# POOL adds three of the eight rows of x, and three pairs of their squares, in three of a kernel's norms

## The chip, the cores and the metric

The kernel runs on one core of one Trainium2 chip. The metric is the device time of one execution in microseconds (us), as the median of several runs. Rows below call the engines PE (TensorE; PEld is its weight load), DVE (VectorE), ACT (ScalarE), POOL (GpSimd) and SP (SyncE, which issues the DMAs).

## The reference

Two stacks of two layers each work on `x` of 256 tokens by 1024 channels, in float32. What matters here is the first stack (`first_block`), which the text calls block 1:

```
for layer in range(DEPTH):                                  # DEPTH = 2
    h = rms_norm(x, norm_mix_pre[layer])
    m = mixer_block(h, ...)                                 # ends in merged @ w_out
    x = x + rms_norm(m, norm_mix_post[layer])
    h = rms_norm(x, norm_ffn_pre[layer])
    f = swiglu(h, w_ffn_gate[layer], w_ffn_up[layer], w_ffn_down[layer])
    x = x + rms_norm(f, norm_ffn_post[layer])

def rms_norm(x, w):
    return x * lax.rsqrt(jnp.mean(x * x, axis=-1, keepdims=True) + EPS) * w
```

Block 2 (`second_block`) takes that x. It normalises x and a context of 256 more tokens, mixes them by a convolution, an mLSTM and attention, and adds the result and a feed-forward to x, in two layers. It begins with the same kind of norm of x as stands behind block 1's mixers.

## The kernel before

**Layout.** The channels lie on the partitions: x is `xs`, 8 rows (k = 0 to 7) of 128 partitions by 512 columns, where columns 0 to 255 are the context of block 2 and 256 to 511 the tokens of x (`LAT`). `mix` and `work` have the same shape. So "a row" below is 128x256 float32, and a sum over channels is a sum over the partitions of all eight rows.

**The weight stream.** All weights come through one ring. SP loads a unit of 128x1024 float32 in two halves into `raw` (3 slots). ACT copies each half to `w_hi` in a rounded format (L1733, semaphore `hi_ready`), and POOL writes the remainder, raw minus w_hi, to `w_lo` (L1065, `lo_ready`); both have 4 slots (`SPLIT`). PE multiplies with w_hi and w_lo (L1114 to L1116, L1130, L1134) and gives a slot free. That is all that POOL does before: 624 units, two halves each, in one loop of 12 units a round (`low_part`, L1061 to L1070). ACT may split unit n only when PE is done with unit n - 4, so POOL has nothing to do while PE takes no new weights.

**A norm between two products** (the places that the change touches) goes like this, in the order in which each engine's program is written out by hand:

1. After the last tile of `w_out` or `w_ffn_down` PE sums the squares of `mix`, ACT takes the root (L1790), DVE the reciprocal (L2229), and PE spreads it over the partitions into a bank, `STAT` (L1243).
2. `add_normed` (DVE, L2386 and L2390): for each row k, work[k] = mix[k] * weight[k] * STAT; then xs[k] = xs[k] + work[k], which counts up `x_ready`. The scaling of row k+1 is written ahead of the addition of row k, and the addition waits (`dve_chain`) for its own scaled row.
3. `squares_of_x` (ACT, L1767): for each row, when `x_ready` says that it is there, work[k] = xs[k] squared, which counts up `sq_ready`. ACT's program is strictly in the order of k.
4. `norm_sums` (PE, L1304 to L1316): per row two matmuls (`token_sums`, L1230; the trace has two records for each) that add the squares over the partitions. `token_sums` waits for `sq_ready` row by row. Behind rows 1, 3 and 5 stands one `modulation_unit` (L1346, four small matmuls on other data) in the two norms behind the mixers; in the norm that begins block 2 there is none, but 4 matmuls of filler (`keep_busy`, L1158) ahead.
5. Root, reciprocal and spreading again, and then DVE, ACT and PE go through the rows of the normalised x into the next product.

The name of the norm tells the place: ("norm_mix_post", 0) and ("norm_mix_post", 1) stand behind block 1's mixers of layer 0 and 1; ("norm_ffn_post", 1) stands behind its last feed-forward and is followed by block 2's first norm. The norm behind layer 0's feed-forward has code of its own and is not touched. Below they are called the first, the second and the third norm.

Of the kernel before, what the change touches and what calls it, by code (L numbers as in the profile page):

```python
# [14 lines left out]
KD = D // P  # L15
# [3 lines left out]
CTX, LAT = (0, SEQ), (SEQ, T2)  # L19
DEPTH = 2  # L20
# [558 lines left out]


PLACE = Place()
FFN2_AT = [next(i for i, t in enumerate(TILES) if t.name == "fa" and t.layer == l) for l in range(DEPTH)]


# [41 lines left out]
def mixer_stack_kernel(nc, stream, vectors, consts, decay, gla_masks, positions, x_in, ctx_in, out):  # L626
# [222 lines left out]
    def sem(name):  # L849
        return nc.alloc_semaphore(name)  # L850
# [25 lines left out]
        sem(n) for n in ("eps_ready", "half_ready", "silu_c_ready")]  # L876

    x_ready = sem("x_ready")

    sq_tile = sem("sq_tile")  # L880
    last_ctx_row = sem("last_ctx_row")
# [112 lines left out]
    with nc.Block() as block:  # L994
# [63 lines left out]
        @block.gpsimd  # L1058
        def _(pool):
            step = RAW * SPLIT  # L1060

            def low_part(unit, before):
                for j, part in enumerate(UNIT_HALVES):
                    pool.wait_ge(hi_ready, before + (j + 1))
                    nc.gpsimd.tensor_tensor(w_lo[:, unit % SPLIT, part], raw[:, unit % RAW, part],  # L1065
                                            w_hi[:, unit % SPLIT, part], ALU.subtract).then_inc(lo_ready, 1)

            with pool.Fori(0, N_UNITS // step) as i:
                for j in range(step):
                    low_part(j, i * (2 * step) + 2 * j)  # L1070
            for unit in range(N_UNITS // step * step, N_UNITS):
                low_part(unit, 2 * unit)


        @block.tensor
        def _(pe):
# [227 lines left out]
            def norm_sums(c0, c1, bank, units=(), spread_bank=None, spare=0):  # L1304
                stat_free()
                keep_busy(bank, spare)
                for unit in units[:-3]:
                    modulation_unit(unit)
                for k in range(KD):
                    E.need(sq_ready)  # L1310
                    last = token_sums(bank, work[:, k, :], c0, c1, k == 0, k == KD - 1)
                    if k % 2 and k // 2 < len(units[-3:]):
                        modulation_unit(units[-3:][k // 2])
                last.then_inc(stat_ready, 1)
                spread_inverse(spread_bank or bank, c0, c1)
# [403 lines left out]
        def _(act):  # L1719
# [49 lines left out]
            def squares_of_x(c0, c1, updated=True):  # L1769
                for k in range(KD):  # L1770
                    if updated:
                        E.need(x_ready)
                    else:
                        act.wait_ge(x_loaded[k * X_PIECES // KD], 16)
                    square(k, xs, c0, c1, sq_ready)

            def root(c0, c1, n, dst=sd, preload=True):

# [436 lines left out]
        def _(dve):  # L2215
# [138 lines left out]
            def add_normed(name, l):  # L2354
# [28 lines left out]
                written = []  # L2383
                for k in range(KD + 1):
                    if k < KD:
                        written.append(C.do(V.scalar_tensor_tensor(work[:, k, c0:c1], mix[:, k, c0:c1], v_(name, l, k),  # L2386
                                                                   STAT[:, c0:c1], MUL, MUL)))
                    if k:
                        C.settle(written[k - 1])
                        V.tensor_tensor(xs[:, k - 1, c0:c1], xs[:, k - 1, c0:c1], work[:, k - 1, c0:c1], ADD)\  # L2390
                            .then_inc(x_ready, 1)
# [118 lines left out]
            c0, c1 = LAT  # L2510
            for l in range(DEPTH):
                if l:
                    dve.wait_ge(x_ready, 2 * KD * l)
                mixer_norm(l)
                if l == 0:
                    dve.wait_ge(vec_loaded, 16)
# [174 lines left out]
                        modulation_at(l, KD * b + f)  # L2691
                merged_low(KD - 1)
                add_normed("norm_mix_post", l)
                dve.wait_ge(x_ready, KD * (2 * l + 1))
                norm1("norm_ffn_pre", l)
                for t in range(NFF + 1):
                    if t < NFF:
# [69 lines left out]
            dve.wait_ge(half_ready, 1)  # L2767
            dve.wait_ge(silu_c_ready, 1)
            dve.wait_ge(ctx_loaded, 16)
            dve.wait_ge(x_ready, 2 * KD * DEPTH)  # L2770
            tapped = {}
            for l in range(DEPTH):
                c0 = 0 if l < DEPTH - 1 else SEQ
# [309 lines left out]
```

## Time and profile before

| | us |
|---|---|
| median of 3 runs (2641.03 to 2645.47) | 2644.31 |
| the profiled execution, its own time | 2644.44 |
| its span, first to last instruction | 2642.3 |
| PE busy | 2603.2 (99% of the span) |
| POOL busy | 1666.2 (63%) |
| DVE busy | 1487.3 (56%) |
| ACT busy | 1340.1 (51%) |

The span is what the trace covers; about 2.1 us of the execution lie outside it. "Busy" is the sum of an engine's instructions, overlaps counted once. TensorE's clock was granted in full for 0.999 of the span. A busy PE is the limit only where its instructions follow each other; in the norms it waits for rows.

### The profile page before, as it was taken

To read this page: it belongs to the slowest core of one execution; us is meant where nothing else is said; L and a number is where in the kernel's file an instruction comes from. 1 tells how busy PE (TensorE), PEld (TensorE's weight loads), DVE (VectorE), ACT (ScalarE), POOL (GpSimd) and SP (SyncE) were. 2 spreads that over 40 slices of the span, in tenths; PEclk is the share of its full clock that TensorE was granted. 3 is DMA by queue.
4 is the path that set the end of the run, shared out by engine and by line. 5 is a ranking of instruction groups with operands and counts; after the bars stand their busy time and mean duration, and the time that the engine had idled before them with its cause. 6 is when DMAs were issued, how large, how long until landed. Compare 5 with 4: busy or idle time off the path is not lost.

```text
span 2642.3 us, 43046 instructions
## 1 busy us (share of the span) xinstructions
PE 2603.2 (99%) x15736; PEld 2243.4 (85%) x15736; DVE 1487.3 (56%) x2545; ACT 1340.1 (51%) x2671; POOL 1666.2 (63%) x1252
## 2 busy tenths in 40 slices
PE   8999999999999999999999999999999999999999
PEld 7998788899888887877788888888888889999888
DVE  6886533388654436855533333668654965235644
ACT  6475545556655553456343343442444575446655
POOL 6779788778887884422334345556554645558887
PEclk9999999999999999999999999999999999999999
DMA  6466676545867552221222223446542423335555
GB/s 220 133 188 209 209 241 190 167 133 160 255 211 223 182 179 91 88 65 56 65 71 80 72 88 114 133 144 225 204 135 85 142 84 109 105 118 161 169 181 162
DMA packets 216445, 386.24 MB, mean 146 GB/s; under 512 B 21952, under 2 KB 49856, under 8 KB 216256
## 3 DMA queue, kind: packets, MB, share of 16 engines
q1 hardware_dynamic: 216256, 383.66, 45.8%
q8 instruction: 126, 2.06, 0.3%
q14 instruction: 63, 0.52, 0.1%
HBM read 382.53 MB, written 1.05 MB: 145 GB/s over the span
## 4 chain that ended last, share of the span: by engine, by line
PE 44%; issue 33%; POOL 17%; DVE 4%; ACT 1%; DMA 0%; POOLq 0%; SPq 0%; DVEq 0%; ACTq 0%
POOL w_lo L1065 17%; PE bank L1130 12%; PE bank L1134 6%; PE bank L1114 6%; PE bank L1116 6%; PE bank L1115 6%; PE bank L1679 1%; PE bank L1230 1%; PE bank L1210 1%; PE bank L1211 1%; PE bank L1212 1%; PE bank L1652 1%; PE bank L1346 1%; DVE k_dec L2604 0%; DVE gdec L2599 0%
## 5 line engine op out<-in xcount | busy, mean ns | idle before, releaser
L1065 POOL TENSOR_TENSOR w_lo<-raw,w_hi 128x512 fp32r<-128x512 f32 x1248 | 1666.0, 1366 | 965.5 <-ACT w_hi L1733 964.4
L1733 ACT ACTIVATE w_hi<-raw 128x512 fp32r<-128x512 f32 x1248 | 719.0, 623 | 295.5 <-PE bank L1116 125.3
L1114 PE MATMUL bank<-hl,w_hi 128*128 128x256 f32 (+1 forms) x1920 | 659.8, 344 | 0.8 <-POOL w_lo L1065 0.3
L1116 PE MATMUL bank<-hl,w_lo 128*128 128x256 f32 (+1 forms) x1920 | 645.4, 336 | 0.0
L1115 PE MATMUL bank<-hl,w_hi 128*128 128x256 f32 (+1 forms) x1920 | 645.2, 336 | 0.0
L1114 PEld LDWEIGHTS bank<-hl,w_hi 128*128 128x128 f32 x1920 | 364.2, 190 | 44.1 <-issue 5.0
L1115 PEld LDWEIGHTS bank<-hl,w_hi 128*128 128x128 f32 x1920 | 364.4, 190 | 40.6 <-issue 3.6
L1116 PEld LDWEIGHTS bank<-hl,w_lo 128*128 128x128 f32 x1920 | 364.2, 190 | 38.0
L1130 PE MATMUL bank<-hl,w_hi 128*128 128x512 f32 x1296 | 361.4, 395 | 0.8 <-POOL w_lo L1065 0.5
L1130 PEld LDWEIGHTS bank<-hl,w_hi 128*128 128x128 f32 x1296 | 221.5, 188 | 31.8 <-issue 3.0
L1134 PEld LDWEIGHTS bank<-hl,w_lo 128*128 128x128 f32 x1296 | 197.7, 188 | 27.6
L1134 PE MATMUL bank<-hl,w_lo 128*128 128x256 f32 x1296 | 205.3, 280 | 0.0
L1130 PE MATMUL bank<-hid,w_hi 128*128 128x512 f32 x462 | 135.0, 397 | 0.0
L1114 PE MATMUL bank<-y,w_hi 128*128 128x256 f32 (+1 forms) x408 | 131.1, 321 | 0.5 <-ACT gate L1756 0.5
L1116 PE MATMUL bank<-y,w_lo 128*128 128x256 f32 (+1 forms) x408 | 129.1, 316 | 0.0
L1115 PE MATMUL bank<-y,w_hi 128*128 128x256 f32 (+1 forms) x408 | 129.0, 316 | 0.0
L2199 ACT ACTIVATE fc<-bank,vec 128x512 f32<-128x512 f32 (+1 forms) x88 | 59.0, 671 | 135.2 <-PE bank L1116 103.3
L2812 DVE SCALAR_TENSOR_TENSOR bank<-z,vec,bank 128x512 f32<-128x512 f32 (+1 forms) x232 | 123.1, 615 | 0.0
L3028 DVE SCALAR_TENSOR_TENSOR fc<-bank,vec,fc 128x510 f32<-128x510 f32 (+1 forms) x88 | 54.1, 615 | 106.0 <-ACT fc L2199 106.0
L1210 PE MATMUL bank<-w_hi,hl 128*128 128x256 f32 x384 | 110.6, 288 | 0.9 <-ACT mv L1763 0.9
L2941 DVE TENSOR_SCALAR wgt<-bank,gcol 128x256 f32<-128x256 f32 (+1 forms) x64 | 31.7, 505 | 139.4 <-PE bank L1679 118.1
L1211 PE MATMUL bank<-w_lo,hl 128*128 128x256 f32 x384 | 108.6, 283 | 0.0
(353 smaller groups left out, 4225.3 us busy)
## 6 DMA issues: line engine op xcount, KB each, us to landing
raw<-stream SPq DMA_DIRECT2D x1248, 256.0 KB, 3.0
mix<-stream SPq DMA_DIRECT2D x64, 512.0 KB, 4.7
spare_lo<-stream SPq DMA_DIRECT2D x16, 512.0 KB, 5.0
spare_hi<-stream SPq DMA_DIRECT2D x16, 512.0 KB, 5.6
xs<-x_rows SPq DMA_DIRECT2D x4, 256.0 KB, 6.0
xs<-ctx_rows SPq DMA_DIRECT2D x1, 1024.0 KB, 6.5
out_rows<-xs SPq DMA_DIRECT2D x8, 128.0 KB, 2.9
dec<-decay SPq DMA_DIRECT2D x1, 768.0 KB, 6.7
```

Of the source, the lines that this page charges most:

```text
L1065: nc.gpsimd.tensor_tensor(w_lo[:, unit % SPLIT, part], raw[:, unit % RAW, part], w_hi[:, unit % SPLIT, part], ALU.subtract).then_inc(lo_re ...
L1114: nc.tensor.matmul(acc, wh, x[:, 0, k, c0:c1], start=k == 0, stop=False)
L1115: nc.tensor.matmul(acc, wh, x[:, 1, k, c0:c1], start=False, stop=False)
L1116: last = nc.tensor.matmul(acc, wl, x[:, 0, k, c0:c1], start=False, stop=k == t.k - 1)
L1130: return nc.tensor.matmul(acc[:, :], w, x[:, :, k, c0:c1], start=k == 0, stop=k == t.k - 1)
L1134: return nc.tensor.matmul(acc[:, 0:SEQ], w, x[:, 0, k, c0:c1], start=False, stop=False)
L1210: nc.tensor.matmul(acc, h_hi[:, k, c:c + P], wh, start=k == 0, stop=False)
L1211: nc.tensor.matmul(acc, h_hi[:, k, c:c + P], wl, start=False, stop=False)
L1733: nc.scalar.activation(w_hi[:, n % SPLIT, part], raw[:, n % RAW, part], ACT.Copy).then_inc(hi_ready, 1)
L2199: nc.scalar.activation(fc[:, t % 2, j, cols], rows, ACT.Identity, bias=v_("ffn_conv_b_2", l, i), scale=v_("ffn_conv_w_2", l, 2 * NFF + i)) ...
L2812: C.do(V.scalar_tensor_tensor(out, z, w, y, MUL, ADD))
L3028: C.do(V.scalar_tensor_tensor(y[:, :, 1:], u[:, :, 0:SEQ - 1], w[0], y[:, :, 1:], MUL, ADD))
```

## The change

POOL, between two of its w_lo halves, does six additions in each of the three norms: rows 0, 2 and 4 of x (`xs += work`, announced on a new semaphore `x_shared` after DVE announces the scaled row on `x_scaled`), and for the pairs (0,1), (2,3), (4,5) work[k] += work[k+1], the sum of two rows of squares (after ACT counts `sq_paired`, announced on `pair_ready`). DVE still scales all eight rows and adds rows 1, 3, 5, 6 and 7. ACT squares all eight rows, in the same order. PE sums 5 rows instead of 8: the three pairs and rows 6 and 7. POOL's loop is cut in four, with straight code between, so that the new additions stand behind the last half that can be split before the norm (`shared_after`).

```
+SHARED_ROWS = range(0, KD - 2, 2)
+SHARED_IN = [("norm_mix_post", 0), ("norm_mix_post", 1), ("norm_ffn_post", 1)]
+def shared_after(name, l):
+    last = [i for i, t in enumerate(TILES) if t.layer == l and (t.array == "w_out" if name == "norm_mix_post" else t.name == "ffd")][-1]
+    return (PLACE.first_block[last] + TILES[last].k * TILES[last].wide - 1) // UNIT + SPLIT - 1
@@ POOL
-            with pool.Fori(0, N_UNITS // step) as i:
-                for j in range(step):
-                    low_part(j, i * (2 * step) + 2 * j)
...
+            def low_parts(first, end):
+                aligned = min(first + -first % step, end)
+                for unit in range(first, aligned):
+                    low_part(unit, 2 * unit)
+                rounds = (end - aligned) // step
+                if rounds > 1:
+                    with pool.Fori(0, rounds) as i:
+                        for j in range(step):
+                            low_part(j, i * (2 * step) + (2 * aligned + 2 * j))
+                    aligned += rounds * step
+                for unit in range(aligned, end):
+                    low_part(unit, 2 * unit)
+            first = 0
+            for n, (name, l) in enumerate(SHARED_IN):
+                c0, c1 = LAT
+                end = shared_after(name, l) + 1
+                low_parts(first, end)
+                rows = len(SHARED_ROWS)
+                for i in range(rows + 1):
+                    if i < rows:
+                        k = SHARED_ROWS[i]
+                        pool.wait_ge(x_scaled, rows * n + i + 1)
+                        nc.gpsimd.tensor_tensor(xs[:, k, c0:c1], xs[:, k, c0:c1], work[:, k, c0:c1], ALU.add)\
+                            .then_inc(x_shared, 1)
+                    if i:
+                        k = SHARED_ROWS[i - 1]
+                        pool.wait_ge(sq_paired, 2 * (rows * n + i))
+                        nc.gpsimd.tensor_tensor(work[:, k, c0:c1], work[:, k, c0:c1], work[:, k + 1, c0:c1], ALU.add)\
+                            .then_inc(pair_ready, 1)
+                first = end
+            low_parts(first, N_UNITS)
@@ PE, norm_sums
                 for k in range(KD):
-                    E.need(sq_ready)
-                    last = token_sums(bank, work[:, k, :], c0, c1, k == 0, k == KD - 1)
+                    if k in SHARED_ROWS:
+                        E.need(pair_ready)
+                    elif k - 1 not in SHARED_ROWS:
+                        E.need(sq_ready)
+                    if k - 1 not in SHARED_ROWS:
+                        last = token_sums(bank, work[:, k, :], c0, c1, k == 0, k == KD - 1)
@@ ACT, squares_of_x
-                        E.need(x_ready)
+                        E.need(x_shared if k in SHARED_ROWS else x_ready)
...
-                    square(k, xs, c0, c1, sq_ready)
+                    square(k, xs, c0, c1, sq_paired if updated and k // 2 * 2 in SHARED_ROWS else sq_ready)
@@ DVE, add_normed
-                        written.append(C.do(V.scalar_tensor_tensor(work[:, k, c0:c1], mix[:, k, c0:c1], v_(name, l, k),
-                                                                   STAT[:, c0:c1], MUL, MUL)))
-                    if k:
+                        row = V.scalar_tensor_tensor(work[:, k, c0:c1], mix[:, k, c0:c1], v_(name, l, k), STAT[:, c0:c1],
+                                                     MUL, MUL)
+                        if k in SHARED_ROWS:
+                            row.then_inc(x_scaled, 1)
+                            written.append(None)
+                        else:
+                            written.append(C.do(row))
+                    if k and k - 1 not in SHARED_ROWS:
```

DVE's later waits for the whole of x (`x_ready`) become one for the rows it adds itself and one for `x_shared`.

DVE's order in the first norm, from the reciprocal before it to the one after, before the change (L2386 scales, L2390 adds):

```order
L2229 RECIPROCAL sd<-sd 128x2 [waits std_ready]
L2386 SCALAR_TENSOR_TENSOR work<-mix,vec,bank 128x256 [waits tile_out,inv_spread]
L2386 SCALAR_TENSOR_TENSOR work<-mix,vec,bank 128x256
L2390 TENSOR_TENSOR xs<-xs,work 128x256 [waits dve_chain]
L2386 SCALAR_TENSOR_TENSOR work<-mix,vec,bank 128x256
L2390 TENSOR_TENSOR xs<-xs,work 128x256 [waits dve_chain]
L2386 SCALAR_TENSOR_TENSOR work<-mix,vec,bank 128x256
L2390 TENSOR_TENSOR xs<-xs,work 128x256 [waits dve_chain]
```

and in the changed kernel (there L2429 scales and L2438 adds; L2272 is the reciprocal):

```order
L2272 RECIPROCAL sd<-sd 128x2 [waits std_ready]
L2429 SCALAR_TENSOR_TENSOR work<-mix,vec,bank 128x256 [waits tile_out,inv_spread]
L2429 SCALAR_TENSOR_TENSOR work<-mix,vec,bank 128x256 x2
L2438 TENSOR_TENSOR xs<-xs,work 128x256 [waits dve_chain]
L2429 SCALAR_TENSOR_TENSOR work<-mix,vec,bank 128x256 x2
L2438 TENSOR_TENSOR xs<-xs,work 128x256 [waits dve_chain]
L2429 SCALAR_TENSOR_TENSOR work<-mix,vec,bank 128x256 x2
L2438 TENSOR_TENSOR xs<-xs,work 128x256 [waits dve_chain]
L2429 SCALAR_TENSOR_TENSOR work<-mix,vec,bank 128x256
L2438 TENSOR_TENSOR xs<-xs,work 128x256 [waits dve_chain] x2
L2272 RECIPROCAL sd<-sd 128x2 [waits std_ready,x_shared,x_ready]
```

Three of eight additions are gone from DVE, those of rows 0, 2 and 4.

POOL's order around the first norm in the changed kernel (L1077 is the w_lo half, L1103 the row of x, L1108 the pair of squares; the first two rows end a loop, the last ones begin the next):

```order
L1086 REGISTER_ALU
L1086 COMPARE_AND_BRANCH
L1077 TENSOR_TENSOR w_lo<-raw,w_hi 128x512 [waits hi_ready] x8
L1103 TENSOR_TENSOR xs<-xs,work 128x256 [waits x_scaled] x2
L1108 TENSOR_TENSOR work<-work 128x256 [waits sq_paired]
L1103 TENSOR_TENSOR xs<-xs,work 128x256 [waits x_scaled]
L1108 TENSOR_TENSOR work<-work 128x256 [waits sq_paired] x2
L1077 TENSOR_TENSOR w_lo<-raw,w_hi 128x512 [waits hi_ready] x16
L1086 UNCONDITIONAL_BRANCH
L1086 ISA
```

Before the change POOL's program was a single loop of w_lo halves with nothing behind it. The order at the second and third norm is the same, with 22 and 10 halves ahead of it and 2 and 14 behind.

PE's order in the first norm in the changed kernel (L1269 sums a row over the partitions, L1389 is the modulation unit):

```order
L1269 MATMUL bank<-cst,work 128x128 [waits pair_ready]
L1269 MATMUL bank<-cst,work 128x128
L1389 MATMUL bank<-mix,silu_c 2x256 [waits ada_loaded3]
L1389 MATMUL bank<-mix,silu_c 2x256 x3
L1269 MATMUL bank<-cst,work 128x128 [waits pair_ready]
L1269 MATMUL bank<-cst,work 128x128
L1389 MATMUL bank<-spare_hi,silu_c 2x256 [waits ada_loaded4]
L1389 MATMUL bank<-spare_hi,silu_c 2x256 x3
L1269 MATMUL bank<-cst,work 128x128 [waits pair_ready]
```

Between two modulation units there now stands one pair where two rows stood; behind the last unit rows 6 and 7 stand as before.

## Rows read from the trace of the kernel before

**Rows 1.** The page: the span, and busy time of each engine
```profile
span 2642.3 us, 43046 instructions
PE 2603.2 (99%) x15736; PEld 2243.4 (85%) x15736; DVE 1487.3 (56%) x2545; ACT 1340.1 (51%) x2671; POOL 1666.2 (63%) x1252
```

**Rows 2.** Timeline of DVE, first norm: start, us, what; [idle before <-releaser]
```profile
298.11 0.87 DVE L2386 SCALAR_TENSOR_TENSOR work<-mix,vec,bank 128x256 f32<-128x256 f32 x2 [0.80 <-PE bank L1243]
298.90 0.42 DVE L2390 TENSOR_TENSOR xs<-xs,work 128x256 f32<-128x256 f32 x1
299.24 0.48 DVE L2386 SCALAR_TENSOR_TENSOR work<-mix,vec,bank 128x256 f32<-128x256 f32 x1
299.63 0.42 DVE L2390 TENSOR_TENSOR xs<-xs,work 128x256 f32<-128x256 f32 x1
...
303.26 0.76 DVE L2390 TENSOR_TENSOR xs<-xs,work 128x256 f32<-128x256 f32 x2
```

**Rows 3.** Timeline of ACT, first norm
```profile
299.35 0.42 ACT L1767 ACTIVATE work<-xs 128x256 f32<-128x256 f32 x1 [2.24 <-DVE xs L2390]
...
303.72 0.75 ACT L1767 ACTIVATE work<-xs 128x256 f32<-128x256 f32 x2 [0.31 <-DVE xs L2390]
306.19 0.26 ACT L1790 ACTIVATE sd<-bank,eps 128x2 f32<-128x2 f32 x1 [1.72 <-PE bank L1230]
```

**Rows 4.** The chain that ended last, from 300.55 to the root at 306.19
```profile
300.55 0.71 PE bank L1230 x4
301.26 0.54 PE bank L1346 x8
301.80 1.09 PE bank L1230 x8
...
304.52 0.54 PE bank L1346 x8
305.07 1.10 PE bank L1230 x8
306.19 0.27 ACT sd L1790
```

**Rows 5.** Timeline of the third norm (begins block 2)
```profile
994.81 0.87 DVE L2386 SCALAR_TENSOR_TENSOR work<-mix,vec,bank 128x256 f32<-128x256 f32 x2 [0.80 <-PE bank L1243]
996.58 5.46 PE L1230 MATMUL bank<-cst,work 128*128 128x128 f32 x32
1000.42 0.75 ACT L1767 ACTIVATE work<-xs 128x256 f32<-128x256 f32 x2 [0.31 <-DVE xs L2390]
1002.08 0.26 ACT L1790 ACTIVATE sd<-bank,eps 128x2 f32<-128x2 f32 x1 [0.91 <-PE bank L1230]
```

**Rows 6.** Timeline of POOL around the first and the third norm
```profile
281.87 15.30 POOL L1065 TENSOR_TENSOR w_lo<-raw,w_hi 128x512 fp32r<-128x512 f32 x12
313.48 2.55 POOL L1065 TENSOR_TENSOR w_lo<-raw,w_hi 128x512 fp32r<-128x512 f32 x2 [16.31 <-ACT w_hi L1733]
...
989.36 5.03 POOL L1065 TENSOR_TENSOR w_lo<-raw,w_hi 128x512 fp32r<-128x512 f32 x4
1010.47 1.29 POOL L1065 TENSOR_TENSOR w_lo<-raw,w_hi 128x512 fp32r<-128x512 f32 x1 [16.08 <-ACT w_hi L1733]
```

**Rows 7.** One line's instructions: duration ns min/median/max, first and last start
```profile
L2390 DVE TENSOR_TENSOR xs<-xs,work x24: 418/419/422, 298.9 to 1000.3; 128x256 f32<-128x256 f32 x24
L2604 DVE TENSOR_TENSOR k_dec<-gqk,gdec x16: 685/1780/1786, 61.4 to 614.5; 128x512 f32<-128x512 f32 x16
L2684 DVE TENSOR_TENSOR mix<-mix,bank x32: 420/420/422, 211.0 to 765.6; 128x256 f32<-128x256 f32 x32
L1065 POOL TENSOR_TENSOR w_lo<-raw,w_hi x1248: 1254/1296/2325, 5.3 to 2630.6; 128x512 fp32r<-128x512 f32 x179
L1065 POOLq MODIFY_POOL_CONFIG  x104: 1/11/63, 0.9 to 2599.2; - x104
```

**Rows 8.** Timeline at 177 us: a DVE addition with POOL idle, and with POOL busy
```profile
177.53 0.42 DVE L2673 SCALAR_TENSOR_TENSOR mix<-gate,branch 128x256 f32<-128x256 f32 x1
...
178.66 2.73 POOL L1065 TENSOR_TENSOR w_lo<-raw,w_hi 128x512 fp32r<-128x512 f32 x2 [2.13 <-ACT w_hi L1733]
179.68 0.56 DVE L2673 SCALAR_TENSOR_TENSOR mix<-gate,branch 128x256 f32<-128x256 f32 x1 [1.06 <-ACT branch L1756]
```

**Rows 9.** Timeline of PE at 2513 us, where POOL was late
```profile
2515.43 0.36 PE L1134 MATMUL bank<-hid,w_lo 128*128 128x256 f32 x1 [1.72 <-POOL w_lo L1065]
2518.36 1.91 PE L1130 MATMUL bank<-hid,w_hi 128*128 128x512 f32 x4
2520.83 1.09 PE L1130 MATMUL bank<-hid,w_hi 128*128 128x512 f32 x4
```

**Rows 10.** Windows: us, busy of PE, PEld, DVE, ACT, POOL (x), PEclk, DMA share, GB/s
```profile
260.00:298.00 38.00, 37.37 (x221) 32.34 (x219) 18.82 (x34) 21.92 (x45) 34.58 (x27) 1.00 0.62 191
298.10:306.20 8.10, 7.70 (x80) 4.69 (x75) 5.91 (x16) 3.26 (x9) 0.00 (x0) 1.00 0.84 257
789.70:797.80 8.10, 7.71 (x80) 4.70 (x77) 5.91 (x16) 3.25 (x8) 0.00 (x0) 1.00 0.83 261
306.20:309.40 3.20, 1.71 (x21) 0.89 (x21) 2.04 (x6) 1.46 (x4) 0.00 (x0) 1.00 1.06 352
994.80:1002.10 7.30, 7.09 (x40) 5.24 (x39) 5.91 (x16) 3.27 (x9) 0.00 (x0) 1.00 0.20 57
2517.30:2520.70 3.40, 3.40 (x13) 3.01 (x12) 0.94 (x2) 1.21 (x3) 3.40 (x4) 0.50 0.41 127
```

More of the change, by code:

```diff
@@ L878, in mixer_stack_kernel @@
     x_ready = sem("x_ready")
+    x_scaled = sem("x_scaled")
+    x_shared = sem("x_shared")
+    sq_paired = sem("sq_paired")
+    pair_ready = sem("pair_ready")
     sq_tile = sem("sq_tile")
@@ L1066, in low_part @@
                                             w_hi[:, unit % SPLIT, part], ALU.subtract).then_inc(lo_ready, 1)
-            with pool.Fori(0, N_UNITS // step) as i:
-                for j in range(step):
-                    low_part(j, i * (2 * step) + 2 * j)
-            for unit in range(N_UNITS // step * step, N_UNITS):
-                low_part(unit, 2 * unit)
+            def low_parts(first, end):
[29 more added lines that the diff above has]
+            low_parts(first, N_UNITS)
         @block.tensor
@@ L2512, in _ @@
                 if l:
-                    dve.wait_ge(x_ready, 2 * KD * l)
+                    dve.wait_ge(x_ready, 2 * KD * l - len(SHARED_ROWS) * l)
+                    dve.wait_ge(x_shared, len(SHARED_ROWS) * l)
                 mixer_norm(l)
@@ L2693, in _ @@
                 add_normed("norm_mix_post", l)
-                dve.wait_ge(x_ready, KD * (2 * l + 1))
+                dve.wait_ge(x_ready, KD * (2 * l + 1) - len(SHARED_ROWS) * (l + 1))
+                dve.wait_ge(x_shared, len(SHARED_ROWS) * (l + 1))
                 norm1("norm_ffn_pre", l)
@@ L2769, in _ @@
             dve.wait_ge(ctx_loaded, 16)
-            dve.wait_ge(x_ready, 2 * KD * DEPTH)
+            dve.wait_ge(x_ready, 2 * KD * DEPTH - len(SHARED_ROWS) * len(SHARED_IN))
+            dve.wait_ge(x_shared, len(SHARED_ROWS) * len(SHARED_IN))
             tapped = {}
```

## The prediction

> **What bounds the kernel now.** I read the page first: PE is busy 99% of the span [rows 1], so a change pays only where PE waits. Then the timeline of each engine through the three norms. In the first, DVE starts its first scaled row at 298.11 and then needs 0.73 us a row, 0.39 for the scaling and 0.34 for the addition, start to start; the last addition ends at 304.02 [rows 2]. ACT's square follows each addition by 0.03 us and takes 0.42; the last ends at 304.47 [rows 3]. PE is later than that: two rows cost 1.09 and a modulation unit 0.54, so from 301.26 on a round of two rows and a unit lasts 1.63 us against 1.46 on DVE, and the last sum ends at 306.17 [rows 4]. So in the first norm (and the second, which has the same program and the same busy times [rows 10]) **PE's own chain ends last**, 8.06 us after the first scaled row. In the third norm there are no units, and **DVE's chain ends last**: from 994.81 the root waits until 1002.08, 7.27 us, right behind the square of row 7, which ends at 1001.17 [rows 5]. POOL is empty in all of this: its last half ends at 297.17 and the next begins at 313.48; around the third norm 994.39 and 1010.47 [rows 6].
>
> **The terms, part by part.** I count from the first scaled row.
>
> *DVE* loses three additions of 0.34 a norm. Alone this would bring its last addition from 5.91 to about 4.95.
>
> *POOL* gains six additions of 128x256 a norm. The trace has no such instruction. The nearest row is the w_lo half of 128x512 at 1.29 us, the same operation of two inputs on twice the columns [rows 6, 7]: half of it, 0.65, is the lower end, the whole of it, 1.29, the upper. I take 0.73, since some 0.17 looks fixed: the half that was held up in rows 8 ended 1.15 us after what held it. In the Trainium skill, "GPSIMD Engine Reference", the table of measured numbers gives 4497 ns for 2048 columns; with 1.29 for 512 that is an estimate of 0.76 us for 256, and the sum below would be about 0.2 us higher.
>
> *POOL and DVE hold each other up.* This is the term that I think decides. A DVE operation with two tensors in SBUF waits for a POOL operation in progress: the same L2673 takes 0.42 us with POOL idle and 0.56 when POOL's half (178.66 to 179.95) runs into it; it ends 0.28 us behind that half, and the next half takes 1.48 instead of 1.29, as the pair of halves shows with 2.73 against 2.55 undisturbed [rows 6, 8]. L2604 has a median of 1.78 us against 0.69 at best [rows 7]. L2684, with one input in a bank of PSUM, never shows it, 420 to 422 ns [rows 7]. Of the norm's operations the scaling has a PSUM input and escapes; the additions of xs and work have two SBUF inputs, always 418 to 422 ns so far because POOL was idle. So POOL's six and DVE's five additions take turns.
>
> With that I wrote out the order by hand (waits cost 0.03 us to ACT, 0.06 to POOL, 0.05 to PE, from the same timelines). POOL adds row 0 from 0.54 to 1.27. Its row 2 could end at 2.06 but comes behind DVE's row 1 (1.19 to 1.61) and ends at 2.19. The pair 0 runs to 2.87; DVE's row 3, ready at 2.32, waits for it and ends at 3.15 instead of 2.74. POOL's row 4 waits for that in turn: 3.73. Pair 2 needs the square of row 3 (3.60) and ends at 4.41; DVE's row 5 waits again and ends at 4.69 instead of 4.28. Its square ends at 5.14, so pair 4 is **ready only at 6.01**; DVE's row 7 waits for it and ends at 6.29, later than the 5.91 of before, and its square at 6.74 instead of 6.36. DVE's gain is gone.
>
> *PE* loses three of eight rows, 3 x 0.545 = 1.6 us of work a norm, but now gets its rows late and in order: it may not sum row 6 before pair 4. First and second norm: pair 4 from 6.06, 0.54 for it, 0.55 for the last unit, 1.09 for rows 6 and 7: 8.24 against 8.06, **+0.18 each**. Third norm: from 6.06 three sums without a unit: 7.69 against 7.24 (the end of the sums), **+0.45**. What was freed on PE is idle time ahead of a wait.
>
> *ACT* has the same eight squares; its rows 0, 2 and 4 now wait for POOL, and rows behind them queue. That is in the sum above. The weight halves are not near: POOL's next begins at 313.48, and its extra work ends 6 us into a gap of 16 [rows 6], so on w_lo it costs nothing; if the cover were gone, it would be six times 0.73 us a norm. The next thing to come late is POOL's last half ahead of the third norm, which ends 0.42 us before the first scaled row and 0.96 before POOL would start its first addition. SP issues the same DMAs in the same order, and none waits for the new semaphores. DVE's split wait for all of x lies ahead of a reciprocal that waits much longer.
>
> The three norms lie one behind another with PE in need of what each produces, and the weights wait in full slots, so a shift here is a shift of the end. **Sum: 0.18 + 0.18 + 0.45 = +0.8 us.** The profiled execution took 2644.44 (span 2642.3 and 2.1 outside), 0.13 above the median of 2644.31; against the median the forecast is 2645.1.
>
> **The rivals.** *A: little contention, a gain.* If DVE gets through first each time and a POOL addition takes 0.65, pair 4 is ready at 5.03, and the sums end at 7.26 in the first two norms and 6.71 in the third: -0.8, -0.8, -0.5, together -2.1 us, 2642.2. The intended 1.0 us of DVE speaks for it, rows 7 and 8 against it. Chance 0.15.
>
> *B: PE's clock falls in a norm.* After the change PE waits from 1.7 (behind the filler in the third norm) to 2.9, from 3.5 to 4.5 and from 5.0 to 6.1. The granted clock was 1.00 (2.4 GHz) throughout the norms of before, also between 306.2 and 309.4 with PE busy 1.71 of 3.2 us [rows 10]; but after PE waited 1.72 us for POOL at 2513.7 it was granted 0.50 (1.2 GHz) for 3.4 us, in which 13 matmuls passed, four of one kind in 1.91 us instead of 1.09 [rows 9, 10]. One such drop takes at most half of 3.4, 1.7 us; one to three drops on top of the forecast give 2646.8 to 2650.2. For it: more idle time than any norm has now. Against it: much of the slow stretch would lie where PE waits anyway. Chance 0.22.
>
> *C: POOL's cut loop comes late with weights; slower.* The loop of 12 units becomes four loops with straight code between, so POOL leaves a loop three times and enters one three times more, in stretches where it is busy 34.6 of 38 us [rows 10]. If each costs POOL a pause that four slots don't cover, PE waits as at 2513.7: 1.72 us and up to 1.2 for the slow clock behind it, 2.9 a time [rows 9]; six times is 17 us, 2662, and it decides from two of the six on (5.8 us, 2650.9). The trace is against it as far as it goes: POOL's jump back stands at the end of each of 52 rounds, and all that is seen there are two instructions of some 11 ns [rows 7]. Chance 0.08. The Trainium skill, "Runtime: NRT & Kernel Launch", section "Instruction fetch mechanics", says that a taken branch whose target isn't in the current window of two pages forces a fetch before execution goes on; by that rule a loop that lies across a page's end could pause in each round, which would be this rival at its worst. No row of before can show it, since its loop was the first thing in the program.
>
> *D: a POOL addition costs the full 1.29.* Then six are 3.4 us longer in each norm: +10 and the 0.8, 2655. The same operation's data part should shrink with the columns; chance 0.03. That the change doesn't do what it says I exclude: the orders show the additions moved, in all three norms.
>
> **How the numbers follow.** Forecast as written 0.52, A 0.15, B 0.22, C 0.08, D 0.03. A measurement of this kernel can tell some 0.2%, 5.3 us, from no change. Forecast and A lie wholly inside, B but for its upper end; C and D mostly outside. Slower by over 0.2%: 0.07 of C, 0.03 of D, 0.01 of B, 0.11. Faster by as much would need more than twice what A can give: 0.02. Same: 0.87. The range starts at A less 0.7 for the spread of the runs (they lie up to 3.3 below the median), 2641.5, and reaches over B, to 2651.0; outside are most of C and D and the tail of the spread.
>
> **What would show it.** Right: POOL's six additions at 0.7 to 0.8 us each, some stretched; DVE's additions of rows 3, 5 and 7 at 0.8 to 0.95 instead of 0.42; PE's last sum at about 8.2 us behind the first scaled row in the first two norms and 7.7 in the third; the rest of the trace shifted, not changed. Wrong, toward A: all DVE additions at 0.42 and last sums before 7.5. Toward B: a granted clock under 1.00 in a window that begins in a norm. Toward C: PE waiting for w_lo near 290, 335, 770, 810, 980 or 1025 us. Beyond that the forecast would be wrong if the norms came out as said and the total moved by more than 2 us, which would mean that a later stretch gives back or adds time.

## The result and the profile after

| | us |
|---|---|
| before, median of 22 runs (2641.03 to 2645.95) | 2643.38 |
| after, median of 22 runs (2645.34 to 2651.68) | 2647.76 |
| ratio, with its 95% interval | 1.0017 [1.0010, 1.0023] |
| the profiled execution of after, its own time (the highest of its 22) | 2651.68 |

The change costs 4.4 us. That is inside the 0.2% that the prediction called no change, and inside its range, but more than five times its sum of 0.8 us. In three of the experiments below one run lay far off the others (3192, 3194 and 8649 us); the ratios leave it out, and without it the medians would be 0.2, 0.03 and 0.3 us lower. The page of the changed kernel answers to [rows 1]:

```profile
span 2649.8 us, 42818 instructions
PE 2602.4 (98%) x15700; PEld 2242.2 (85%) x15700; DVE 1490.6 (56%) x2536; ACT 1340.3 (51%) x2671; POOL 1677.5 (63%) x1270
```

DVE lost nine additions and is busier than before by 3.3 us; PE lost 36 records and is less busy by only 0.8 us. The norms explain part of it: DVE is busy 6.30 to 6.33 us in each instead of 5.91, together 1.2 us more. The rest of DVE's 3.3 says nothing about the change: the kernel of the first experiment, in which no addition moved, has 2.2 more than before as well. These are lines of the changed kernel's timeline through the first norm (start, us, what; [idle before <-releaser]), which answer to [rows 2, 3]; lines between them are left out:

```profile
299.49 1.26 DVE L2429 SCALAR_TENSOR_TENSOR work<-mix,vec,bank 128x256 f32<-128x256 f32 x3 [0.80 <-PE bank L1282]
300.05 1.62 POOL L1103 TENSOR_TENSOR xs<-xs,work 128x256 f32<-128x256 f32 x2 [1.63 <-DVE work L2429]
301.63 0.72 POOL L1108 TENSOR_TENSOR work<-work 128x256 f32<-128x256 f32 x1
301.79 0.85 DVE L2438 TENSOR_TENSOR xs<-xs,work 128x256 f32<-128x256 f32 x1
302.32 0.91 POOL L1103 TENSOR_TENSOR xs<-xs,work 128x256 f32<-128x256 f32 x1
302.41 0.71 PE L1269 MATMUL bank<-cst,work 128*128 128x128 f32 x4 [1.55 <-POOL work L1108]
303.34 0.85 DVE L2438 TENSOR_TENSOR xs<-xs,work 128x256 f32<-128x256 f32 x1
...
304.51 1.29 DVE L2438 TENSOR_TENSOR xs<-xs,work 128x256 f32<-128x256 f32 x2
304.72 0.79 POOL L1108 TENSOR_TENSOR work<-work 128x256 f32<-128x256 f32 x1 [0.81 <-ACT work L1810]
305.57 0.71 PE L1269 MATMUL bank<-cst,work 128*128 128x128 f32 x4 [0.34 <-POOL work L1108]
306.75 1.16 PE L1269 MATMUL bank<-cst,work 128*128 128x128 f32 x8
307.95 0.26 ACT L1833 ACTIVATE sd<-bank,eps 128x2 f32<-128x2 f32 x1 [1.70 <-PE bank L1269]
```

DVE and POOL take turns at SBUF, the memory in which `xs` and `work` lie: DVE's row 3 (301.79) stands for 0.85 us, until 0.29 after POOL's pair (ends 302.35); POOL's row 4 is stretched behind it to 0.91. Pair 4 is ready at 305.51, 6.02 us after the first scaled row; the last addition ends at 305.80, which is 6.31, where it was 5.91 before. The chain that ended last shows the pair in it, as [rows 4] did the rounds of PE:

```profile
304.23 0.42 ACT work L1810
304.66 0.07 issue
304.72 0.80 POOL work L1108
305.52 0.04 issue
305.57 0.71 PE bank L1269 x4
306.28 0.54 PE bank L1389 x8
306.82 1.10 PE bank L1269 x8
```

The three lines' durations over all three norms (ns, min/median/max), beside [rows 7]:

```profile
L2438 DVE TENSOR_TENSOR xs<-xs,work x15: 410/846/951, 300.7 to 1004.1; 128x256 f32<-128x256 f32 x15
L1103 POOL TENSOR_TENSOR xs<-xs,work x9: 731/845/907, 300.0 to 1001.6; 128x256 f32<-128x256 f32 x9
L1108 POOL TENSOR_TENSOR work<-work x9: 719/729/788, 301.6 to 1004.0; 128x256 f32<-128x256 f32 x9
```

So far the norm is the one that was forecast. The second and the third are not. Windows (us, busy of PE, PEld, DVE, ACT, POOL, granted clock, DMA share, GB/s), beside [rows 10]: the first norm, the second, and the stretch from inside the third norm into block 2:

```profile
299.50:307.90 8.40, 6.20 (x68) 3.27 (x60) 6.30 (x13) 3.22 (x8) 4.61 (x6) 1.00 0.81 270
792.20:801.70 9.50, 7.64 (x68) 3.86 (x60) 6.29 (x13) 3.23 (x8) 4.61 (x6) 0.82 0.87 279
1005.20:1012.00 6.80, 6.15 (x23) 5.26 (x22) 2.51 (x7) 2.02 (x5) 0.00 (x0) 0.50 0.00 0
```

The second norm has the same 68 matmul records as the first, and PE is busy 1.44 us longer with them. The granted clock was 0.50 (1.2 GHz) for 3.4 us from 797.0, and for 6.8 us from 1005.2. A third low stretch, at 2524.1, is the one that the kernel before has at 2517.3 [rows 10]. PE's first two sums in the second norm, and its timeline of the third, in part:

```profile
795.11 0.71 PE L1269 MATMUL bank<-cst,work 128*128 128x128 f32 x4 [1.56 <-POOL work L1108]
796.66 1.00 PE L1269 MATMUL bank<-cst,work 128*128 128x128 f32 x4 [0.30 <-POOL work L1108]
...
1001.72 0.71 PE L1269 MATMUL bank<-cst,work 128*128 128x128 f32 x4 [1.27 <-POOL work L1108]
1003.27 0.71 PE L1269 MATMUL bank<-cst,work 128*128 128x128 f32 x4 [0.84 <-POOL work L1108]
1004.86 2.69 PE L1269 MATMUL bank<-cst,work 128*128 128x128 f32 x12 [0.88 <-POOL work L1108]
...
1009.22 1.91 PE L1197 MATMUL bank<-cst 128*128 128x256 f32 x4
```

PE waits 1.27, 0.84 and 0.88 us for three pairs, and then the clock halves; in the second norm it waited 1.56 and 0.30 us ahead of the drop. From the first scaled row to the start of the root the norms take 8.46, 9.56 and 8.83 us; before it was 8.08, 8.08 and 7.27. Together that is 3.4 us. About 1.3 more come behind the third norm, where the clock is still at half: block 2's first group of products on L1220 (L1181 before) starts 5.22 us behind the start of the root instead of 3.94.

### The profile page after: what moved, and what is told of

Read it like the earlier page. It is cut to its first block, busy times and chain, and to the rows that moved or that the text cites. A ratio compares the mean times of both kernels' runs of the same rounds, so it can differ in the third digit from the quotient of the medians.

```text
span 2649.8 us, 42818 instructions
## 1 busy us (share of the span) xinstructions
PE 2602.4 (98%) x15700; PEld 2242.2 (85%) x15700; DVE 1490.6 (56%) x2536; ACT 1340.3 (51%) x2671; POOL 1677.5 (63%) x1270
## 4 chain that ended last, share of the span: by engine, by line
PE 39%; issue 34%; POOL 20%; DVE 4%; ACT 1%; DMA 1%; POOLq 0%; SPq 0%; DVEq 0%; ACTq 0%
POOL w_lo L1077 20%; PE bank L1169 9%; PE bank L1153 6%; PE bank L1154 6%; PE bank L1155 6%; PE bank L1173 4%; PE bank L1722 1%; PE bank L1249 1%; PE bank L1250 1%; PE bank L1251 1%; PE bank L1269 1%; PE bank L1695 1%; DVE k_dec L2653 0%; DVE gdec L2648 0%; DMA raw<-stream 0%
## 5 line engine op out<-in xcount | busy, mean ns | idle before, releaser
L1077 POOL TENSOR_TENSOR w_lo<-raw,w_hi 128x512 fp32r<-128x512 f32 x1248 | 1663.5, 1366 | 954.8 <-ACT w_hi L1776 954.3
```

## The experiments

Diffs are against the changed kernel and in part; "..." marks what is left out. All times below are medians of 11 runs (12 of the change again), each beside 20 to 35 runs of the kernel before on the same chip; the first four experiments ran on one chip, the others on another. The norm lengths are from each profiled execution, from first scaled row to start of the root. My theory after the result: the turns at SBUF and the pairs that come late by them add some 1.2 us, the fallen clock the rest. Rivals: the cut loop of POOL costs; or the waits as such cost, the clock does not matter.

**The cut loop alone.** POOL's loop cut in four as in the change, and nothing else:

```diff
-                rows = len(SHARED_ROWS)
-                for i in range(rows + 1):
...
-                            .then_inc(pair_ready, 1)
...
-                        if k in SHARED_ROWS:
-                            row.then_inc(x_scaled, 1)
-                            written.append(None)
...
```

> The kernel before with POOL's loop cut into the same four loops and straight code, and no addition moved. Theory (the norms and the clock in them carry the 4.4 us): 2643.4, within 1 us of before, and the chain up to the first norm as long as before. Rival C (the cut loop makes POOL late with w_lo): 2645 to 2648, with PE waiting for w_lo near 61, 275 and 570 us, where the profiled run of the change came out 1.4 us later before any norm.

Measured: 2643.24 against 2643.49, ratio 0.9997 [0.9988, 1.0006]; norms 8.08, 8.08, 7.26. The cut costs nothing that can be measured (the interval reaches from -3.2 to 1.6 us).

**Rows alone.** POOL adds rows 0, 2 and 4 of x, but no pairs; PE sums eight rows as before:

```diff
-                    if i:
-                        k = SHARED_ROWS[i - 1]
-                        pool.wait_ge(sq_paired, 2 * (rows * n + i))
-                        nc.gpsimd.tensor_tensor(work[:, k, c0:c1], work[:, k, c0:c1], work[:, k + 1, c0:c1], ALU.add)\
-                            .then_inc(pair_ready, 1)
...
```

> POOL adds rows 0, 2 and 4 of x only; PE sums eight rows of squares again. Theory of turns at SBUF: DVE's additions of rows 3 and 5 may still wait for POOL's rows 2 and 4, but no pair stands behind them, so DVE ends at about 5.2 us behind the first scaled row; PE has its eight rows again and ends at about 8.0 in the first two norms and 6.6 in the third (7.27 before), and with no long idle stretch on PE the clock stays up: 2642.5 to 2643.5, before or a little less. Rival (POOL's additions of x themselves are what costs): 2645 or more.

Measured: 2640.81 against 2643.49, 0.9989 [0.9980, 0.9998]; norms 7.89, 7.89, 6.26. It is faster than the kernel before, and by more than I expected. DVE's additions are short again, and in the third norm PE sums all eight rows without a pause (both from this kernel's trace, the lines and the timeline):

```profile
L2430 DVE TENSOR_TENSOR xs<-xs,work x15: 415/417/420, 298.7 to 998.3; 128x256 f32<-128x256 f32 x15
L1103 POOL TENSOR_TENSOR xs<-xs,work x9: 724/844/847, 298.1 to 996.3; 128x256 f32<-128x256 f32 x9
```

```profile
993.82 1.26 DVE L2421 SCALAR_TENSOR_TENSOR work<-mix,vec,bank 128x256 f32<-128x256 f32 x3 [0.80 <-PE bank L1277]
995.67 4.38 PE L1264 MATMUL bank<-cst,work 128*128 128x128 f32 x32 [0.16 <-ACT work L1802]
```

While one of POOL's three operations is in progress DVE scales, with one input in PSUM, the banks that PE writes; its additions begin when POOL has 0.11 us or less to go, or has ended. POOL's second and third do start beside a DVE addition and take 0.84 instead of 0.72; the norm is shorter all the same. Six POOL operations do not fit in this way.

**Pairs alone.** DVE adds all eight rows, POOL sums the three pairs:

```diff
-                        pool.wait_ge(x_scaled, rows * n + i + 1)
-                        nc.gpsimd.tensor_tensor(xs[:, k, c0:c1], xs[:, k, c0:c1], work[:, k, c0:c1], ALU.add)\
-                            .then_inc(x_shared, 1)
...
```

> POOL adds only the three pairs of squares; DVE adds all rows of x. Theory: each pair holds up one DVE addition by up to 0.6 us and PE waits for pairs: the last sum at about 7.6 us in the first two norms (5 sums instead of 8, against 8.06 before) and 7.3 in the third, but idle stretches on PE remain, so some clock drops: 2643 to 2646. If the clock drop follows from PE's summing three rows less, this kernel has drops as well, and the one with rows only has none.

Measured: 2650.26 against 2643.49, 1.0026 [1.0017, 1.0035]; norms 9.56, 9.98, 9.41. I had expected at most 2646. Most of DVE's additions are short here, as their line shows. Of the eight in the first norm three take longer, 0.55, 0.56 and 0.95 us, and the last ends 6.73 us behind the first scaled row, where it was 5.91 before and 6.31 in the change. This is the slowest kernel of all: the clock fell in all three norms, at 301.8, 796.7 and 1004.9. The line, PE's first sum in the first norm, and the windows of the first and third:

```profile
L2428 DVE TENSOR_TENSOR xs<-xs,work x24: 411/418/949, 299.1 to 1004.1; 128x256 f32<-128x256 f32 x24
301.62 1.11 PE L1264 MATMUL bank<-cst,work 128*128 128x128 f32 x4 [1.93 <-POOL work L1103]
```

```profile
301.80:305.20 3.40, 3.40 (x24) 1.78 (x24) 3.25 (x8) 1.79 (x5) 1.58 (x2) 0.50 0.99 303
1004.90:1008.30 3.40, 2.83 (x12) 2.53 (x12) 0.32 (x2) 0.68 (x2) 0.00 (x0) 0.50 0.00 0
```

This profile lies 1.8 us below its kernel's median. It also lacks the low stretch near 2520 us that every other profile has, though PE waits there for w_lo as ever (1.74 us, 1.72 in the kernel before). From the start of the third norm's root to the end it takes 1638.8 us, the kernel before 1640.2.

**The change with PE kept busy.** Filler matmuls into an idle bank ahead of each wait for a pair; everything else as in the change:

```diff
...
                     if k in SHARED_ROWS:
+                        keep_busy(idle, ((3, 1, 1) if units else (2, 2, 2))[k // 2])
                         E.need(pair_ready)
```

> The change with filler matmuls on PE ahead of each pair's sum (3, 1, 1 in the first two norms, 2, 2, 2 in the third), into a bank that is free. Theory (of 4.4 us some 1 is the turns at SBUF and 3.4 the clock falling in or behind the second and third norm): no granted clock under 1.00 in the norms, 2644.4, about 3 us less than the change. Rival (the clock costs nothing, the rest is elsewhere): 2647.8 or more, since filler only adds work.

Measured: 2644.29 against 2643.49, 1.0003 [0.9994, 1.0012]; norms 8.55, 8.54, 7.77, clock at 1.00 in all of them. More work on PE makes the change 3.5 us faster. PE's timeline of the third norm, beside the one of after above, and two windows, from ahead of the sums to behind them:

```profile
997.74 0.71 PE L1269 MATMUL bank<-cst,work 128*128 128x128 f32 x4 [0.41 <-POOL work L1108]
998.28 1.03 PE L1197 MATMUL bank<-cst 128*128 128x256 f32 x4
...
1000.89 1.60 PE L1269 MATMUL bank<-cst,work 128*128 128x128 f32 x12
```

```profile
994.80:1002.50 7.70, 7.26 (x40) 5.55 (x38) 6.32 (x13) 3.23 (x8) 4.65 (x6) 1.00 0.16 54
1002.50:1009.00 6.50, 5.61 (x26) 4.44 (x27) 5.09 (x14) 3.21 (x7) 0.00 (x0) 1.00 0.01 3
```

The last twelve records take 1.60 us instead of 2.69, and DVE is busy 6.32 us as in the change (6.33 in its third norm): the turns are still there, the fallen clock is not. By the medians that leaves 0.8 us (its interval is -1.6 to 3.2) for the turns and the late pairs, and 3.5 for the clock. The runs without a profile agree: the mean granted clock of an execution is 0.997 to 0.999 in the 22 runs of the change, and 0.999 or 1.000 in each of the 33 runs of the three kernels with filler.

**The change without the turns.** DVE writes its own scaled rows to a bank of PSUM, so that its additions have only one input in SBUF. The bank holds two rows, so ahead of each further one DVE waits until its own addition has read the place:

```diff
+                            dve.wait_ge(x_ready, before + own.index(k) - 1)
...
-                        V.tensor_tensor(xs[:, k - 1, c0:c1], xs[:, k - 1, c0:c1], work[:, k - 1, c0:c1], ADD)\
+                        V.tensor_tensor(xs[:, k - 1, c0:c1], scaled_row(k - 1), xs[:, k - 1, c0:c1], ADD)\
```

> The change, but DVE's own scaled rows (1, 3, 5, 6, 7) are written to a free bank of PSUM, so that its additions have one input in SBUF and one in PSUM; POOL's work is the same. Theory of turns at SBUF: all 15 DVE additions at 0.42 us or less and POOL's at 0.73, pair 4 ready about 0.5 us earlier; norms of 7.8 us (first, second) and 7.2 (third) where the clock holds, against 8.5 and 7.75 for the change. PE still waits for pairs, so the clock can still fall: 2644 to 2647. Rival (DVE's additions wait for POOL for another reason, such as a semaphore): additions stay at 0.85 us.

Measured: 2644.88 against 2643.34, 1.0004 [0.9996, 1.0013]; norms 9.37, 7.86, 7.96. The second is at full clock, and 0.60 us shorter than the undisturbed norm of the change. The lines of the additions, DVE's and POOL's, at the same time as each other as before:

```profile
L2448 DVE TENSOR_TENSOR xs<-bank,xs x15: 411/415/417, 298.4 to 1000.4; 128x256 f32<-128x256 f32 x15
L1109 POOL TENSOR_TENSOR xs<-xs,work x9: 722/728/737, 297.8 to 998.6; 128x256 f32<-128x256 f32 x9
```

No addition is lengthened any more, on either engine. The clock fell again, at 301.5 and 1001.3, where PE still waits for pairs. By the medians the kernel is still 1.5 us above the one before, which the interval doesn't separate from none. The drop in the first norm came behind a single long wait of PE (its first two sums):

```profile
300.11 0.71 PE L1275 MATMUL bank<-cst,work 128*128 128x128 f32 x4 [1.55 <-POOL work L1114]
...
301.49 1.22 PE L1275 MATMUL bank<-cst,work 128*128 128x128 f32 x4
```

In the second norm PE waits 1.54 us in the same place, and the clock holds.

**Both remedies.** The PSUM rows and filler together:

```diff
...
+                        keep_busy(idle, ((2, 0, 1) if units else (2, 1, 1))[k // 2])
```

> The same with filler on PE ahead of the pairs (2, 0, 1 in the first two norms, 2, 1, 1 in the third), which takes both suspected costs away. Theory: no low clock in the norms, norms of 7.8, 7.8 and 7.2 us: 2642.5 to 2643, before less 0.5, and still above the kernel that shares rows only (2640.8), because pairs come late whatever is done. Rival (pairs are worth having once nothing contends): 2641 or less.

Measured: 2642.98 against 2643.34, 0.9999 [0.9990, 1.0008]; norms 8.28, 8.28, 6.86, clock at 1.00. The first two miss what I expected by 0.5: beside the modulation units the filler is in the way. Pair 4 of the first norm is ready at 5.11 us, but PE comes to its sum only at 6.01, straight from the filler. So this kernel does not show the pairs at their best, and it is level with the one before. An estimate of their best takes 7.86 from the undisturbed second norm of the last kernel, twice, and 6.86 from the third norm here: 22.6 us, against 23.4 before and 22.0 with rows alone. Even then the pairs would only lose some of what the rows gain.

**Rows alone, again, on the chip of the last two:**

> The kernel that shares rows only, once more, on the same chip as the two above and the change. Norms of 7.89, 7.89 and 6.26 us add up to 1.4 us less than before; if the norms are all there is to it the median is 1.4 below before, if its 2.7 of the first measurement was real it is 2.7 below.

Measured: 2641.77 against 2643.34, 0.9991 [0.9982, 0.9999]; norms 7.89, 7.89, 6.26 as at first. The norms give 0.19 + 0.19 + 1.01 = 1.4 us, the two measurements 2.7 and 1.6; whether the first has more than scatter in it stays open. Both intervals lie below 1, if barely.

**The change itself, again:**

> The change itself again, beside the others on one chip: 4.4 us above before. Its trace shows where the clock falls in another execution: the contention theory wants the same DVE and POOL durations in all three norms; the clock theory wants low clock in or right behind norms, but not necessarily the same ones as in the first trace.

Measured: 2648.61 against 2643.34, 1.0017 [1.0008, 1.0026]; norms 8.45, 8.46, 9.07. This time the clock fell in the third norm only (and at 64.2, behind a wait of 2.11 us for DVE that has nothing to do with the change; the kernel before waits 1.77 there, and the first profile of the change 2.88, both without a drop). Two windows, the third norm and the low stretch:

```profile
996.80:1005.80 9.00, 6.01 (x28) 4.80 (x26) 6.30 (x13) 3.22 (x8) 4.63 (x6) 0.84 0.11 40
1002.80:1006.20 3.40, 2.93 (x12) 2.63 (x12) 0.30 (x1) 0.68 (x2) 0.02 (x1) 0.51 0.00 0
```

So the same program loses the clock in one norm or another from one execution to the next, with the same waits. This goes with its wider spread, 6.3 us over the 22 runs of the result against 4.9 before: the seven runs with a mean granted clock of 0.997 took 2647.8 to 2651.7 us, the five with 0.999 2645.3 to 2647.6.

**Pairs alone with PE kept busy:**

```diff
...
+                        keep_busy(idle, ((3, 1, 1) if units else (3, 2, 2))[k // 2])
```

> The kernel that shares the pairs only, with filler on PE ahead of each pair (3, 1, 1 and 3, 2, 2). The first such kernel without filler took 6.8 us more than before with low clock in all three norms. If the clock is the larger part, this one has none and stands 1 to 2.5 us above before (pair 4 is ready at 6.4 us, norms near 8.6, 8.6 and 8.1). Rival (late pairs alone cost 6.8): 2649 or more.

Measured: 2644.40 against 2643.32, 1.0006 [0.9997, 1.0015]; norms 8.92, 8.92, 8.14, clock at 1.00. The 6.8 us of pairs alone shrink to 1.1. The norms are longer by 0.84, 0.84 and 0.87 than before, 2.5 in all; the interval of the total, -0.8 to 4.0 us, has room for that. The profile gives none of it back behind the norms: its span is 1.9 us longer than before, 2.5 from the norms less 1.0 by which it reaches the first norm earlier, plus 0.3 elsewhere, and profiles differ by more than that ahead of the first norm (296.1 to 299.5 us to the first scaled row, over all of them).

**The rows and one pair.** Only rows 0 and 1 are paired, and PE sums that pair and six rows:

```diff
...
-                    if k in SHARED_ROWS:
+                    if k == 0:
                         E.need(pair_ready)
-                    elif k - 1 not in SHARED_ROWS:
+                    elif k > 1:
                         E.need(sq_ready)
...
```

> POOL adds rows 0, 2 and 4 of x as in the change, but only the first pair of squares; PE sums seven rows. One pair is late by 1.1 us at PE's first sum and saves one row's 0.55: by hand the norms are 8.4, 8.4 and 6.8 us against 7.89, 7.89 and 6.26 without it, so +1.5 us on the kernel with rows only: 2642.8 to 2643.5, about before. If the clock falls it does so rarely, since PE has no second and third gap. Rival (pairs help where only one is taken): 2641 or less.

Measured: 2644.30 against 2643.32, 1.0001 [0.9992, 1.0011]; norms 8.56, 8.56, 6.73. The first sum on PE waits 1.55 us for the pair, then everything runs without a gap, and the clock holds (PE's timeline, first norm):

```profile
300.81 0.71 PE L1269 MATMUL bank<-cst,work 128*128 128x128 f32 x4 [1.55 <-POOL work L1108]
301.45 0.61 PE L1389 MATMUL bank<-mix,silu_c 128*2 128x256 f32 x8
301.99 1.16 PE L1269 MATMUL bank<-cst,work 128*128 128x128 f32 x8
```

Even the pair that is ready first makes the norms longer than with rows alone, by 0.67, 0.67 and 0.47 us: PE can't start before the pair is there, and from then on its own rounds of 1.63 us set the end. The wait of 1.55 us did not bring the clock down in this execution; the change has the same wait, and further ones behind it. That one such wait is never enough is not shown: in the first norm of the change without the turns it was.

## Why the prediction was right or wrong

**Right: nearly the whole order written out by hand.** POOL's operation took 0.72 to 0.73 undisturbed (forecast 0.73). DVE's additions of rows 3, 5 and 7 took 0.85 to 0.95 (0.8 to 0.95). Pair 4 was ready at 6.02 (6.01), the last addition ended at 6.31 (6.29). That two SBUF inputs are what matters is shown, not only inferred: with one input in PSUM the additions take 0.41 to 0.42 and the norm is 0.60 shorter. One small slip: three additions of 0.34 off 5.91 are 4.89, not 4.95, and 4.89 is where DVE ends with rows alone. The Trainium skill, "GPSIMD Engine Reference", section "Key points", says that POOL contends with DVE instructions that have two SBUF inputs; the traces agree, with 846 ns against 415 for one addition.

**A term too small: PE's sum behind a wait.** "Pair 4 from 6.06, 0.54 for it": the chain above has 0.71 for those four records, which come behind a wait; within a stream on PE four take 0.54. [rows 4] already had 0.71 in its first line. So an undisturbed first or second norm grows by 0.38, not 0.18. The third would be 8.83 less the 1.09 that twelve records lose at half the clock (2.69 against 1.60), 7.74: +0.47, with 0.45 forecast. The sum at full clock is then 0.38 + 0.38 + 0.47 = 1.2 us instead of 0.8. The change with filler is 0.8 above before, its interval from -1.6 to 3.2 us: the runs do not tell 1.2 from 0.8, and the norms of the traces say 1.2.

**The choice that failed: rival B was the case, not the forecast.** Its mechanism, its place and its size were in the text (2646.8 to 2650.2; measured 2647.76). Those figures stood on 2644.31, the median of 3 runs; over 22 runs before is 2643.38, so the forecast would be 2644.2 and B 2645.9 to 2649.3, which changes nothing in this. But B was given 0.22 because "much of the slow stretch would lie where PE waits anyway". It doesn't. In the change the clock falls behind the second or third wait, so the slow stretch covers the last sums, which nothing hides: 1.10 us in the second norm, 1.09 in the third, and about 1.3 behind it, in the filler (four matmuls in 1.91 instead of 1.03) and block 2's first products. That is 3.5 us in the profiled execution, which is the slowest of its 22, and filler on PE alone takes 3.5 of the 4.4 away. That the total still came out inside the stated 0.2% is owed to the width of that band, not to the sum. The text had the list of PE's gaps (1.7 to 2.9, 3.5 to 4.5, 5.0 to 6.1) and the one row where a gap of 1.72 had cost the clock; it should have weighed that three norms now have several of them in a row.

**Rival A (little contention)** falls: the additions do wait, as the forecast had it. **Rival C (the cut loop)** falls by its own experiment, 0.9997. The rule that the prediction cited for it from the Trainium skill, "Runtime: NRT & Kernel Launch", section "Instruction fetch mechanics", has no effect here that can be measured. **Rival D** falls with 0.73 for a POOL addition.

**The marks.** The one toward B, a granted clock under 1.00 in a window that begins in a norm, was seen. The last one asked whether the total moves by more than the norms do, and it did: 7.5 us between the spans of the two profiles against 3.4 in the norms. 1.3 of the rest is the low clock behind the third norm. 1.4 lies ahead of the first norm, where nothing but POOL's loop has changed; the profiles of all twelve kernels reach their first scaled row between 296.1 and 299.5 us, so that is scatter. Some 0.7 arises between the first and the second norm and 0.7 near 2520 us; their cause stays open. The profiled execution is also 3.9 us above its kernel's median. For the median itself there is only an estimate. At full clock the norms cost 1.2 us, which leaves 3.2 of the 4.4 for the clock; a stretch of 3.4 us cost 1.1 to 1.3 in the norms of the profiles. Ten of the 22 runs, the median among them, have a mean granted clock of 0.998, which is about 10.6 us at half clock, two stretches more than the one of before and, as the mean is rounded, perhaps three. That is 2.2 to 3.9 us.

## What to carry to other kernels

In this kernel work that goes to POOL was free only while DVE's instructions beside it did not have two inputs in SBUF: three additions ran beside DVE's scalings and gained 1.6 to 2.7 us by the medians, 1.4 by the norms; the next three made DVE wait, and POOL after it. Fewer matmuls are no gain when each comes behind a longer wait: ask whether PE still gets its inputs without a gap, because a few short gaps can cost the clock for the matmuls behind them, and these are the ones that end the chain. The version to keep is rows alone: 2640.8 and 2641.8 us in two measurements, below both kernels (2643.4 and 2647.8).

## What was unexpected of the hardware

- Two SBUF-input operations of DVE and POOL lengthen each other by up to a whole instruction: in the change a DVE addition of 128x256 that starts well inside one of POOL's ends 0.28 to 0.29 us behind it and takes 845 to 951 ns instead of 418 to 422, and POOL's own goes from 722 to as much as 907.
- The clock fell to 0.50 after quite short waits of PE: 1.27, 0.84 and 0.88 us between sums of 0.71 in the third norm, 1.56 and 0.30 in the second. Where the pairs came without filler and without turns, one wait of 1.55 us was enough in the first norm and one of 1.54 was not in the second; in the kernel with one pair the clock stayed at 1.00 in all norms with the same wait. What exactly decides between these the runs don't tell.
- Whether it falls differs between executions of one program: in the second norm in one, not in the other, with POOL busy 4.61 and 4.60 us and DVE 6.31 and 6.30. Likewise PE's wait of 1.68 to 1.75 us for w_lo near 2520 us was followed by a low stretch in eleven of the twelve profiles, and by none in the kernel with pairs alone. A single profile of such a kernel tells the size of a drop, not how often it comes.
- In these runs a low stretch lasted 3.4 us, or twice that.
